# Decay exponentials moved out of the recurrence's start, constant tables loaded after the activations, filler matmuls at two stage edges and a reordered end of the late mixers

## The reference, cut to what matters

```python
z = x @ w_in                                   # layer 1: 1824 columns for RWKV, 1536 for MoBA
z = z + (shift(z) - z) * shift_mix             # token shift
decay = exp(-exp(w));  w = -softplus(-(w0 + tanh(w_d) @ w_up)) - 0.5
S = S * decay + (S @ a) b^T + v k^T;  y = S @ r            # per token and head, RWKV-7
y_a = (groupnorm(y) * lnx_g + lnx_b + bonus) * g
...
h = num / max(abs(den), exp(-m))               # layer 3, mLSTM output
h = headwise_rms_norm(h, gain) * sigmoid(o)
mix = concat(y_a, y_b, y_c, y_d) @ w_out
```

## Time and profile before

| | |
|---|---|
| Median of 3 runs | 2229.1 us (2228.11 to 2233.07) |
| Profiled execution | 2233.85 us, span 2232.1 us |
| TensorE busy, mean granted clock | 2120.5 us (95%), 0.983 |
| VectorE, ScalarE, GpSimd busy | 1241.0, 821.6, 262.7 us |
| Instructions | 30634 |
| DMA | 179.23 MB, mean 80 GB/s |

### The profile page before, as it was taken

How to read it: one execution, slowest core, us unless ns; L and a number is a source line. 1 busy time by engine, 2 the same in 40 slices (tenths; PEclk the granted TensorE clock), 3 DMA queues, 4 the chain that set the end, 5 groups by cost and what they waited for, 6 DMA issues and landing times. The chain is left out here.

```text
span 2232.1 us, 30634 instructions
## 1 busy us (share of the span) xinstructions
PE 2120.5 (95%) x12530; PEld 1692.8 (76%) x12530; DVE 1241.0 (56%) x1704; ACT 821.6 (37%) x1294; POOL 262.7 (12%) x268
## 2 busy tenths in 40 slices
PE   7999999999999989999999999999998789999996
PEld 5776986778887778888778788877665567878875
DVE  5546766642343466666573444458768637533544
ACT  3343423531242344444452323335234544222221
POOL 0000001000000100000110890020552010000002
PEclk9999999999999999999999999999999999999998
DMA  6121002222222222222123222323111042223321
GB/s 218 65 68 37 3 4 79 85 101 94 95 95 85 76 76 76 76 68 74 40 96 100 90 95 95 100 84 129 67 54 37 2 142 85 88 83 114 100 71 64
DMA packets 51675, 179.23 MB, mean 80 GB/s; under 512 B 5784, under 2 KB 5784, under 8 KB 51280
## 3 DMA queue, kind: packets, MB, share of 16 engines
q1 hardware_dynamic: 47712, 165.45, 22.4%
q10 hardware_dynamic: 3328, 8.13, 1.0%
q0 software_dynamic: 496, 3.69, 0.4%
HBM read 172.51 MB, written 4.21 MB: 79 GB/s over the span
## 5 line engine op out<-in xcount | busy, mean ns | idle before, releaser
L1126 DVE TENSOR_TENSOR w_lo<-w_raw,w_hi 128x1024 fp32r<-128x1024 f32 (+1 forms) x320 | 411.8, 1288 | 730.5 <-ACT w_hi L1119 730.4
L1224 PE MATMUL banks<-xh,w_hi 128*128 128x512 f32 x1560 | 625.9, 401 | 4.6 <-PEq L213 3.6
L1226 PE MATMUL banks<-xh,w_lo 128*128 128x512 f32 x1560 | 610.3, 391 | 0.0
L1225 PE MATMUL banks<-xl,w_hi 128*128 128x512 f32 x1560 | 610.2, 391 | 0.0
L1119 ACT ACTIVATE w_hi<-w_raw 128x1024 fp32r<-128x1024 f32 (+1 forms) x320 | 328.6, 1029 | 720.2 <-PE banks L1226 686.3
L1224 PEld LDWEIGHTS banks<-xh,w_hi 128*128 128x128 f32 x1560 | 294.8, 189 | 84.0 <-issue 20.5
L1226 PEld LDWEIGHTS banks<-xh,w_lo 128*128 128x128 f32 x1560 | 294.2, 189 | 63.4
L1225 PEld LDWEIGHTS banks<-xl,w_hi 128*128 128x128 f32 x1560 | 294.8, 189 | 58.8 <-issue 1.7
L1224 PE MATMUL banks<-hh,w_hi 128*128 128x512 f32 x688 | 272.0, 395 | 11.7 <-DVE w_lo L1126 4.8
L1225 PE MATMUL banks<-hl,w_hi 128*128 128x512 f32 x688 | 269.5, 392 | 0.0
L1226 PE MATMUL banks<-hh,w_lo 128*128 128x512 f32 x688 | 269.5, 392 | 0.0
(11 more groups left out here) (509 smaller groups left out, 2655.9 us busy)
## 6 DMA issues: line engine op xcount, KB each, us to landing
w_raw<-in_w SPq DMA_DIRECT2D x128, 512.0 KB, 3.4
w_raw<-in_w_gu SPq DMA_DIRECT2D x44, 512.0 KB, 3.4
w_raw<-in_w_c_in SPq DMA_DIRECT2D x40, 512.0 KB, 3.4
w_raw<-in_w_ab_in SPq DMA_DIRECT2D x27, 512.0 KB, 3.4
w_raw<-in_w_in SPq DMA_DIRECT2D x25, 512.0 KB, 3.4
w_raw<-in_w_down SPq DMA_DIRECT2D x16, 384.0 KB, 3.0
w_raw<-in_w_down SPq DMA_DIRECT2D x16, 320.0 KB, 2.8
w_raw<-in_w_ab_out SPq DMA_DIRECT2D x8, 512.0 KB, 3.4
```

What stands on the lines that cost most here:

```text
L1126: dve.tensor_tensor(lo[:, 0:n], core.raw[u % RAW][:, 0:n], hi[:, 0:n].bitcast(F32), ALU.subtract).then_inc(core.split_ready, 1)
L1224: pe.matmul(bank, hi[:, w], src.xh[:, kk, :], start=kk == 0, stop=False)
L1225: pe.matmul(bank, hi[:, w], src.xl[:, kk, :], start=False, stop=False)
L1226: mm = pe.matmul(bank, lo[:, w], src.xh[:, kk, :], start=False, stop=last)
```

## The change

Five edits. (1) The eight exponentials move from the head of ScalarE's queue in `rwkv` to `RwkvInputs.act` at j = 26, ahead of the four gate copies; AR is placed by the program at the start of region S, over xh, at the address that it had, and the stage's other tiles begin behind it as before. (2) `outer` issues `keep_busy(..., 3)` at its start for split sources other than the first. (3) POOL's memsets come before, and its transfers of consts and masks after, a wait for the sixth tile of x. (4) In the late mixers, VectorE's `divide(1)` comes before `scale(3)`. (5) There TensorE gets `keep_busy(core, pe, 4, 5)` before its last sum and `keep_busy(core, pe, 4, 3)` behind it.

```diff
@@ RwkvInputs.act @@
         if j == 26:
+            act.wait_ge(s.before, 1)
+            for c in range(4):
+                act.activation(self.AR[:, c, :, 0, :], self.lw[:, c, :].rearrange("p (n t) -> p n t", t=C), ACT.Exp, scale=-DECAY).then_inc(s.e_before, 1)
+            for c in range(4):
+                act.activation(self.AR[:, c, :, 1, :], self.cum[:, c, :].rearrange("p (n t) -> p n t", t=C), ACT.Exp, scale=-DECAY).then_inc(s.e_in, 1)
             for c in range(4):
                 act.wait_ge(s.gate_in, c + 1)
@@ Chain.outer @@
+        if part.u0 and isinstance(src, Split):
+            keep_busy(core, pe, SHIFT_BANK, 3)
         for k in range(KD):
@@ rwkv @@
-    with Stage(core, "rwkv", end=end_of("W") - 4 * TILE) as st:
-        AR = st.sb("AR", [P, 4, NCH, 2, C])
+    with Stage(core, "rwkv", at=at_of("S") + 8 * TILE, end=end_of("W") - 4 * TILE) as st:
...
         @block.scalar
         def _(act):
-            for c in range(4):
-                act.activation(at[:, c], chunked(lw)[:, c], ACT.Exp, scale=-DECAY).then_inc(s.e_before, 1)
-            for c in range(4):
-                act.activation(rt[:, c], chunked(cum)[:, c], ACT.Exp, scale=-DECAY).then_inc(s.e_in, 1)
             for q in range(12):
...
             dve.tensor_tensor(bonus, core.banks[:, 3:7, :], v, ALU.mult).then_inc(s.bonus_ready, 1)
-            dve.wait_ge(s.e_before, 4)
             dve.scalar_tensor_tensor(at, chunked(kk), -1.0, at, ALU.mult, ALU.mult).then_inc(s.at_ready, 1)
-            dve.wait_ge(s.e_in, 4)
@@ late_mixers @@
             mlstm.limit(dve, 1)
+            mlstm.divide(dve, 1)
             norms.scale(dve, 3)
-            mlstm.divide(dve, 1)
             norms.gate(dve, 7)
...
             mlstm.heads(pe, 15)
+            keep_busy(core, pe, 4, 5)
             norms.total(pe, 7)
+            keep_busy(core, pe, 4, 3)
@@ load_and_project, pool @@
             gp.dma_start(core.params[:, 0:PARAM_N], core.io["params"]).then_inc(core.params_in, 16)
+            for n, v in (("eps_ln", LN_EPS), ("eps_gn", GN_EPS), ("eps_rms", RMS_EPS)):
+                gp.memset(core.param(n), v).then_inc(s.set_eps, 1)
+
+            gp.wait_ge(x_in[5], 16)
             gp.dma_start(core.consts[:], core.io["consts"]).then_inc(core.consts_in, 16)
             gp.dma_start(masks[:], core.io["masks"]).then_inc(core.consts_in, 16)
-            for n, v in (("eps_ln", LN_EPS), ("eps_gn", GN_EPS), ("eps_rms", RMS_EPS)):
-                gp.memset(core.param(n), v).then_inc(s.set_eps, 1)
             gp.wait_ge(core.consts_in, 32)
```

More of the change, by code:

```diff
@@ L604, with __init__ @@
 class RwkvInputs:
-    def __init__(self, core, st, Z, small, norm, gate, shift, moba):
+    def __init__(self, core, st, Z, small, norm, gate, AR, shift, moba):
         self.core, self.Z, self.shift, self.moba, self.norm = core, Z, shift, moba, norm[:]
-        self.small, self.gate = small, gate
+        self.small, self.gate, self.AR = small, gate, AR
         Y = core.Y
@@ L617, in __init__ @@
         self.s = st.sems("rate_in decay_in kk_sum rk_sum tanhed gate_sig rate decay squared log inv e_neg "
-                         "kk_raw rate_less k_new cum clamped rk before kk_unit b scaled gate_in gate_out", "inputs_")
+                         "kk_raw rate_less k_new cum clamped rk before kk_unit b scaled gate_in gate_out e_before e_in", "inputs_")
     def rate(self, pe, c, bank):
@@ L1299, with rwkv @@
 DECAY = float(np.exp(-0.5))
-def rwkv(core, Z, O, gate):
+def rwkv(core, Z, O, gate, AR):
     nc, Y = core.nc, core.Y
@@ L1335, in rwkv @@
         XT = chunked(Y[:, 0:4, :])
-        s = st.sems("e_before e_in elast_kept at_ready rt_ready bonus_ready "
+        s = st.sems("elast_kept at_ready rt_ready bonus_ready "
                     "tok tok_out zeroed b_diag k_diag b_pairs k_pairs masked x_first "
@@ L3265, with load_and_project @@
 RWKV_ORDER = (12, 13, 14, 4, 5, 6, 7, 0, 1, 2, 3, 8, 9, 10, 11)
-def load_and_project(core, Z, O, small, norm, gate):
+def load_and_project(core, Z, O, small, norm, gate, AR):
     with Stage(core, "load") as st:
@@ L3280, in load_and_project @@
         shift = Shift(Z, LINE_AT(4), RWKV_ORDER, core.params_in, tiles)
-        inputs = RwkvInputs(core, st, Z, small, norm, gate, shift, moba)
+        inputs = RwkvInputs(core, st, Z, small, norm, gate, AR, shift, moba)
         segments = [(12, tiles), (15, shift)]
@@ L3439, in program @@
         gate = place("rwkv_gate", [P, 4, T], end_of("W") - 4 * TILE)
-        load_and_project(core, Z, O, small, norm, gate)
-        rwkv(core, Z, O, gate)
+        AR = place("rwkv_AR", [P, 4, NCH, 2, C], at_of("S"))
+        load_and_project(core, Z, O, small, norm, gate, AR)
+        rwkv(core, Z, O, gate, AR)
         first_layers(core, O)
```

## The result

The changed kernel takes 2221.28 us (median of 6 runs, 2218.95 to 2221.82); the kernel before, run beside it, takes 2232.1 (6 runs, 2228.11 to 2237.18). The ratio is 0.9948 [0.9936, 0.996], so 11.6 us less on 2232.1, where 11.1 had been forecast (a time of 2218 us, between 2212 and 2225). The three runs known before the prediction had been at the low end; in later series the kernel before takes 2233.25 to 2233.87.

The account below looks back on a forecast made before the run. TensorE, busy 95% of the span, bounds the kernel; only its waits or half clock can pay. Terms 5.3 + 0 + 2.0 + 2.4 + 1.4 = 11.1 us, taken from the median 2229.1, give 2218 us, range 2212 to 2225.

Parts of the forecast that it names:

- Tables, -5.3: Kernel start: with constants and masks sent later, x lands earlier and unit 2 starts at 22.8, not 28.16; 5.3 us saved.
- Their landing near 21 to 27.7: Kernel start: the delayed tables are in at about 21 us, or at 27.7 at their old pace.
- the slack: Projection: the tables are late only from about 28, leaving 0.3 us at the worst pace, 7 at the likely one.
- the deciding point: Projection: tables landing at 39 us would eat the whole gain; rival of late tables and a slower kernel, 4%.
- Exponentials, 0: Projection to recurrence: moving eight activations off the recurrence's start gains nothing, as TensorE's run of 384 matmuls sets it.
- The latest point that the sum allowed: Projection's end: exponentials starting no sooner than 219.1 would still be done at 225.3, in time for the last gate copy.
- Filler at the first output product, -2.0: Recurrence's output product: keep_busy(3) keeps the clock up, so slice 2 starts at 356.67, not 358.69; 2.0 us saved.
- The two short pauses that it was to leave: First output product: the pause from 349.8 to 352.5 becomes two of 0.4 and 0.9 us.
- Mixers' end, -2.4: Late mixers' end: earlier division and a sum at full clock, less TensorE's filler ending 0.4 late; 2.4 us saved.
- the second filler, -1.4: Feed-forward's start: filler ahead of its product brings slice 2 3.8 us earlier, 1.4 beyond the mixers' 2.4.
- The rival "fillers run cold": All filler places: at 1.2 GHz three calls take 5.3 us, giving 2229 us in total; chance 7%.
- The second rival, clock falls elsewhere: Later pauses of 2 to 4 us: each clock fall costs some 1.6 us; three more 2223, three fewer 2213; 10%.

Follow-up runs that it names:

- e11: Changed kernel plus five float32 matmuls of zeros on TensorE before its first product; 0.9936, 2219.41 us.
- e10: Changed kernel with the tables' transfers waiting for three used units instead of the sixth tile of x; 1.0001, 2233.38 us.
- e2: Kernel before with only the eight exponentials moved; gain in ratio -0.0005, read as nothing.
- e3: Kernel before with only keep_busy(3) ahead of the two output products; gained 6.2 us (4.2 to 8.5).
- e8: Changed kernel with the late mixers' end as before (old order, neither filler there); lost 2.7 us against the whole change rerun.
- e12: Changed kernel plus the zero matmuls at the start, and two keep_busy calls instead of three behind the mixers' last sum; 0.993, 2217.2 us.
- e9: Changed kernel without the last keep_busy(3) of the late mixers; 0.9947, 2220.76 us.
- e5: The changed kernel run again, whole, against the kernel before; ratio 0.9941, a gain of 13.2 us.
- e7: Changed kernel without keep_busy(3) ahead of the two output products; ratio 0.9979.
- e4: Kernel before with only the late mixers' part (division first, fillers before and behind the last sum); ratio 1.0011.
- e1: Kernel before with only the tables' transfers moved behind the sixth tile of x; gained 2.2 us, not clear of noise.

## Why the prediction was right, point by point

**Tables, -5.3: right in kind, too large.** Unit 2 starts 4.6 us sooner in the pair of profiles, and the load stretch is 4.1 shorter on the mean of eleven. Arrival of x was no longer a limit, as said. What was off is the pace: the slices were counted at full clock from 14.6, a rise read from one execution of before in which it came at 13.9; after the change it came within the row of 15.44, so more matmuls took the half-clock distance of 0.43 us. That is most of the 0.75 us between 22.8 and 23.55. e11, which has the clock up from the first slice on, shortens the start by 2.3. Their landing near 21 to 27.7 held (23.7), the slack too, and e10 puts the price and the deciding point where the sum had them.

**Exponentials, 0: right,** by e2 and by the unchanged 11.41 and 1.94. They begin at 213.11. The latest point that the sum allowed, 219.1 by the times of before, is 214.5 by those of after (the last gate copy starts at 220.85 and not 225.41), so the slack was 1.4 us. That the copies behind them wait for TensorE is seen in their releaser.

**Filler at the first output product, -2.0: right** (1.6 to 2.1 at its place, in nine profiles with it and five without). The two short pauses that it was to leave, 0.4 and 0.9 us, are there, with 0.41 and 0.80.

**Mixers' end, -2.4, and the second filler, -1.4: right together,** 3.8 against 3.6 to 3.8. But the prediction wrote them as two terms, and they are one. With the first alone 1.0 to 1.2 come, for the pause ahead of the product then costs a fall of the clock, which before the change was already paid; with the second alone 0.5, since it runs cold. The rival "fillers run cold" is thus what happens in e3 and e8, and what doesn't happen where the filler ahead has kept the clock up. That TensorE's own filler is late next, by 0.4, was right (0.66 measured), and shortening it by one call (e12) gives that back; leaving it out (e9) gives back about half of it.

**The sum.** The terms seen at their places are 4.1 + 0 + 2 + 3.7, or 9.8 us; the measured difference is 11.6 [8.9, 14.3] there and 13.2 in e5. Alone, the parts show 4.1 + 0 + 2 + 1.1 + 0.5, or 7.7, at the same places, so their being one chain at the mixers' end explains 2.1 us of the 8.3 by which the whole beats their sum (intervals of some 3 to 5 us lie on both). The rest lies outside of these places, and no term of the prediction has it. The second rival, clock falls elsewhere, is what the profiles show there.

So that 11.1 and 11.6 agree so well is in part luck: the tables' term was 1.2 us too large, and about 2 us came from outside of the four places. The forecast of 2218 also leaned on the low median of three runs.

Falls elsewhere come and go by chance. The changed kernel itself shows it in its two profiles: after has 182.2 and 65.0 us in the two stretches from 1965.7 to 2212.9, e5 has 183.8 and 63.4. So 124.18 against 122.55, or 51.84 against 53.05, in stretches that no edit touches, prove nothing for a single pair.

Over all executions it is not chance alone. The fillers ahead of the two products gain more than their two stretches show, in both comparisons: 6.2 us (at least 4.2) in e3 against 2.6 at the two places, and 8.5 (at least 5) from e7 to e5 against 4.4. That leaves some 4 us each time. The mean granted clock of all executions says the same: span times (1 - clock) is 37 to 38 us before, 31 in e3, 34 in e7 and 25 in e5. **Open:** where these 4 us lie. With one profile for each kernel it can be counted only roughly: the stretch from 1568.0 has its longer form, 124.1, in four of the five profiles without these fillers and in two of the nine with them. Open too is why e4's total is some 3.5 us worse than its stretch (a loss of 2.4 against a gain of 1.1).

## What to carry to other kernels

Ask of a large transfer that is issued early who needs it first: two tables of 2.6 MB moved behind six of eight tiles halved those tiles' landing time, and the price comes at once when their first reader has to wait. Fillers at stage edges belong in a chain: each must start while the clock is still up and end before the real work is due, so judge them together; alone, one of two showed a seventh of what both gave (0.5 of 3.7). And take an edit's worth from the stretch in which it stands, over several executions, as well as from the total: the totals of e1 to e4 lay 1 to 4 us off what their own stretches showed, and in e3 and e7 that difference was itself an effect of the edit.

## What the runs showed of the hardware that was not expected

- A fall of the clock has a nearly fixed price in dense work, 1.4 to 1.6 us, and comes or stays out at the same place from one profile to the next (with the same kernel too, 65.0 or 63.4 from 2147.9 on): 12.41 or 13.9 (the run of 384), 122.6 or 124.1, and among the stretches summed as rest 30.76 or 32.34, 82.66 or 84.26, 182.2 or 183.8. The Trainium skill (TensorE: Matmul & The Clock Gate, section "What's actually happening") says of a kernel's start that the count of slow matmuls varies from run to run; these profiles show the like far behind the start.
- The clock falls also when TensorE is at work again: in e4 the matmul of 1788.81, behind a pause of 3.12 us, takes 0.50 us, and only that of 1790.54 takes 0.80; in e2 it is at 0.99 from 226 to 228 and at 0.50 from 228 on, so it falls as the run of 64x64 matmuls begins at 227.87, right behind a pause of 0.99. The prediction had held pauses of under 1 us harmless. Here they mostly were, but in three of fourteen profiles the run that follows this one starts with a fall.
- Matmuls of zeros raise the clock: with ten steps of them from 1.46 us on, the product's first matmul, at 8.87, takes 0.50 us; without them it takes 0.80 at 8.85, and the clock rises only within the row of 15.44.
